# The pairs of experts of a mixture-of-experts stage written out, and the steps around a gated block put ahead of the weight splits

## The reference

```python
def moe_swiglu(x, router, w_gate, w_up, w_down):
    logits = (x @ router).astype(jnp.float32)
    top_vals, top_idx = lax.top_k(logits, TOP_K)            # 2 of 8 experts for each token
    gates = jax.nn.softmax(top_vals, axis=-1)
    combine = jnp.sum(jax.nn.one_hot(top_idx, N_EXPERTS) * gates[..., None], axis=-2)
    y = jnp.zeros_like(x)
    for e in range(N_EXPERTS):                              # w_gate[e], w_up[e]: 1024 x 3584
        y = y + combine[..., e:e + 1] * swiglu(x, w_gate[e], w_up[e], w_down[e])
    return y                                                # w_down[e]: 3584 x 1024
```

## Time and profile before

| | |
|---|---|
| median of 3 runs | 1626.28 us (1620.76, 1626.28, 1626.63) |
| the profiled execution | 1621.89 us, its span 1620.2 us |
| busy in the span | PE 94%, PEld 78%, DVE 78%, ACT 64%, POOL 8% |
| mean granted TensorE clock | 0.981 of full speed |
| traffic | 484 MB, of which HBM read 477 MB; 303 GB/s over the span |

### The profile page before, as it was taken

One profiled execution on the slowest core, in us unless ns is written; L12 is line 12 of the kernel. 1 busy time (PEld: TensorE's weight loads), 2 busy tenths in 40 slices (PEclk: granted clock), 3 DMA queues, 4 the chain that ended last, 5 costly groups with the idle time before them and its releaser, 6 DMA issues.

```text
span 1620.2 us, 21958 instructions
## 1 busy us (share of the span) xinstructions
PE 1517.1 (94%) x7866; PEld 1266.3 (78%) x7866; DVE 1257.4 (78%) x1228; ACT 1042.0 (64%) x984; POOL 126.8 (8%) x148
## 2 busy tenths in 40 slices
PE   9999999999999998899998999888999989999786
PEld 9888988888896797788776787776887766887664
DVE  5687475554647666789889989789988989988987
ACT  4574444443436453677888777888776978777664
POOL 3103010000104201000000000000000000000220
PEclk9999999999999999999999999999999999999888
DMA  9448856465565462799999999999999999999994
GB/s 355 167 131 247 299 185 218 130 221 195 169 198 184 140 208 75 268 374 340 412 403 409 409 376 383 350 403 391 410 365 382 355 403 386 405 358 385 346 368 152
DMA packets 164690, 484.28 MB, mean 299 GB/s; under 512 B 8352, under 2 KB 11456, under 8 KB 164576
## 3 DMA queue, kind: packets, MB, share of 16 engines
q1 hardware_dynamic: 155504, 454.06, 75.2%
q0 software_dynamic: 7440, 25.83, 4.9%
q10 hardware_dynamic: 1632, 2.88, 0.5%
HBM read 477.21 MB, written 13.92 MB: 303 GB/s over the span
## 4 chain that ended last, share of the span: by engine, by line
PE 61%; DVE 17%; issue 13%; ACT 5%; DMA 3%; POOL 1%; ACTq 0%; DVEq 0%; POOLq 0%
PE bank L428 8%; PE bank L430 8%; PE bank L429 8%; PE bank L461 7%; PE bank L463 6%; PE bank L462 6%; DVE w_lo L2200 6%; ACT w_hi L1232 3%; PE bank L451 2%; PE bank L454 2%; PE bank L453 2%; DMA c_add<-gate_rows 2%; DVE w_lo_more L2200 2%; DVE w_lo L1643 1%; PE bank L424 1%
## 5 line engine op out<-in xcount | busy, mean ns | idle before, releaser
L1232 ACT ACTIVATE w_hi<-raw 128x2048 fp32r<-128x2048 f32 (+1 forms) x322 | 606.7, 1894 | 224.9 <-PE bank L463 105.5
L2200 DVE TENSOR_TENSOR w_lo<-raw,w_hi 128x2048 fp32r<-128x2048 f32 x221 | 502.8, 2287 | 62.4 <-ACT w_hi L1232 55.7
L1643 DVE TENSOR_TENSOR w_lo<-raw,w_hi 128x2048 fp32r<-128x2048 f32 (+1 forms) x96 | 211.1, 2203 | 144.4 <-ACT w_hi L1232 144.0
L2200 DVE TENSOR_TENSOR w_lo_more<-raw,w_hi_more 128x2048 fp32r<-128x2048 f32 x63 | 144.0, 2285 | 17.6 <-ACT w_hi_more L1232 14.6
L461 PE MATMUL bank<-w_hi,xT_hi 128*128 128x512 f32 (+1 forms) x384 | 147.1, 383 | 0.1
L424 PE MATMUL bank<-w_hi,xe_two 128*128 128x512 f32 x304 | 128.3, 422 | 19.6 <-DVE w_lo L2200 19.1
L463 PE MATMUL bank<-w_hi,xT_lo 128*128 128x512 f32 (+1 forms) x384 | 144.6, 377 | 0.0
L462 PE MATMUL bank<-w_lo,xT_hi 128*128 128x512 f32 (+1 forms) x384 | 144.5, 376 | 0.0
L1232 ACT ACTIVATE w_hi_more<-raw 128x2048 fp32r<-128x2048 f32 x64 | 122.5, 1914 | 13.4 <-PE bank L430 8.4
L425 PE MATMUL bank<-w_lo,xe_two 128*128 128x512 f32 x304 | 124.5, 410 | 1.6 <-issue 1.5
L428 PE MATMUL bank<-w_hi,xe_hi 128*128 128x512 f32 x304 | 120.8, 397 | 1.9 <-DVE xe_lo L2033 1.7
(11 more groups left out here) (374 smaller groups left out, 3177.7 us busy)
## 6 DMA issues: line engine op xcount, KB each, us to landing
raw<-in_moe_w_gate_dram SPq DMA_DIRECT2D x112, 1024.0 KB, 8.0
raw<-in_moe_w_down_dram SPq DMA_DIRECT2D x96, 1024.0 KB, 7.9
raw<-in_moe_w_up_dram SPq DMA_DIRECT2D x80, 1024.0 KB, 8.5
raw_more<-in_moe_w_up_dram SPq DMA_DIRECT2D x32, 1024.0 KB, 8.3
raw<-in_mem_wkv_dram SPq DMA_DIRECT2D x16, 1024.0 KB, 5.2
raw_more<-in_moe_w_down_dram SPq DMA_DIRECT2D x16, 1024.0 KB, 7.6
raw<-in_c_w_in_dram SPq DMA_DIRECT2D x12, 1024.0 KB, 5.1
raw<-in_ffn_w_gate_dram SPq DMA_DIRECT2D x10, 1024.0 KB, 5.6
```

The source lines that it names most:

```text
L1232: return nc.scalar.activation(dst, src, ACT.Copy)
L1643: tt(w_lo[s][:, 0:n], raw[c % NRAW][:, 0:n], w_hi[s][:, 0:n].bitcast(F32), ALU.subtract).then_inc(lo_made, 1)
L2200: tt(w_lo[s][:, :], raw_exp[r][:, :], w_hi[s][:, :].bitcast(F32), ALU.subtract).then_inc(lo_made, 1)
```

## The change

It rewrites how the pairs are run; the arithmetic is the same.

- The loop over pairs is a Python loop: the six jobs stand one behind the other in the program of PE, ACT, DVE and POOL. `job` is `wide + 2 * i`, where `wide` is still read at run time. The loop around the first wide job stays.
- Within the pairs and z the slots go round by four without a break: 84 chunks of a pair are a multiple of four, and the w job starts two slots on (`slot_of`). Each step c splits exactly chunk c + 4 (`splits`).
- ACT and DVE do the steps of a gated block ahead of the step's splits. The multiplication itself returns the bank; the last subtraction counts up a semaphore `eT_two_made` of its own, for which PE's down projection waits.
- The table is loaded at the start of the first kind of job only.
- Turned tokens are written only in the form that the next job reads: `xe_hi`/`xe_lo` from an n job, `xe_two` from a w job.
- At the end of an n job ACT does the two copies; DVE adds one bank there and the other in step 1 of the w job. The write of these rows moves from step 2 to step 4, and the PE product that looks up the next tokens (line 857) from step 4 to step 6.

```diff
+        def slot_of(z, n):
+            return E_SLOT[n % EC if z == "" else (n + 2 * (z == "w")) % (NSPL + 1)]
+
+        def splits(z, c):
+            return E_SPLIT[c] if z == "" else [c + NSPL + 1]
-        C_WIDE_Y = 2
+        C_WIDE_Y = 4
-        C_INDEX, C_TURN, C_COMBINE = 4, 4 * EJ + 4, 4 * EJ + EK // CK + 2
+        C_INDEX, C_TURN, C_COMBINE = 6, 4 * EJ + 4, 4 * EJ + EK // CK + 2
...
-            with pe.Fori(0, PAIRS) as i:
-                job = pe.snap(wide + 2 * i)
-                expert(job, "n", True)
+            for i in range(PAIRS):
+                job = wide + 2 * i
+                expert(job, "n", True, i)
                 expert(job + 1, "w", False)
...
+                            if narrow:
+                                pe.wait_ge(sem("eT_two_made"), EJ * n_narrow + q // 2 + 1)
+                            else:
+                                wait_emptied(pe, f"{z}et{q // 2}", job)
...
-                nc.scalar.preload_act_table_set("silu_and_others")
+                if z == "":
+                    nc.scalar.preload_act_table_set("silu_and_others")
...
+                    if z == "n" and c == EC - 1:
+                        act.wait_ge(chunk_used, idx + 1)
+                        for i in (1, 0):
+                            act.wait_ge(sem(f"y_kept{i}"), 16 * job + 16)
+                            copy(y[0:HP, i * W:(i + 1) * W], bank_of(f"{z}ed{i}")[HP:P, :])\
+                                .then_inc(sem(f"y_low{i}"), 1)
...
-                    for n in E_SPLIT[c]:
-                        if n < EC or not last:
-                            w_split(n)
                     if c in C_HID:
...
                     if narrow and c in C_LOW:
-                        act.wait_ge(sem("e_mult"), EJ * n_narrow + j + 1)
+                        wait_emptied(act, f"{z}et{j}", job)
...
+                    for n in splits(z, c):
+                        if n < EC or not last:
+                            w_split(n)
...
-                        tt(e_mul[j % 2][:, :], bank_of(f"{z}et{j}")[:, W // 2:W], e_act[j % 2][:, :], ALU.mult)\
-                            .then_inc(sem("e_mult"), 1)
+                        empties(tt(e_mul[j % 2][:, :], bank_of(f"{z}et{j}")[:, W // 2:W], e_act[j % 2][:, :],
+                                   ALU.mult), f"{z}et{j}")
```

More of the change, by code:

```diff
@@ L885, in combine, with expert @@
                         .then_inc(filled[2 * half + t], 1)
-            def expert(job, z, narrow):
+            def expert(job, z, narrow, n_narrow=None):
                 claims[:], signals[:] = before[0], before[1]
@@ L1208, in _ @@
                 next_x(job)
-            with pool.Fori(0, PAIRS) as i:
-                job = pool.snap(wide + 2 * i)
+            for i in range(PAIRS):
+                job = wide + 2 * i
                 next_x(job)
@@ L1503, in _, with turned @@
             nc.scalar.activation(gap[:, :], gap[:, :], ACT.Exp).then_inc(sem("gap_exp"), 1)
[L1505 removed]
+            def turned(tag, job, z):
                 for half in range(2):
                     b = wait_filled(act, f"{tag}{half}", job)
[L1508 to L1514 removed]
+                    if z in ("", "w"):
+                        ins = copy(xe_two[:, 4 * half:4 * half + 4, 0:HP],
+                                   b[:, :].rearrange("p (k s) -> p k s", k=4)[:, :, 0:HP])
+                    if z != "w":
+                        ins = copy(xe_hi[:, 4 * half:4 * half + 4, :].rearrange("p k s -> p (k s)"), b[:, :])
+                    ins.then_inc(sem("xe_hi_made"), 1)
+            turned("xA", None, "first")
             split(N0 + NSPL)
@@ L1602, in _ @@
                 expert(job, "", False)
-            with act.Fori(0, PAIRS) as i:
-                job = act.snap(wide + 2 * i)
+            for i in range(PAIRS):
+                job = wide + 2 * i
                 expert(job, "n", True, i)
@@ L2021, in indexed, with turned @@
                 copy(got_i[:, :], b[:, 0:1]).then_inc(sem("index_made"), 1)
-            def turned(tag, job):
+            def turned(tag, job, z):
                 for half in range(2):
@@ L2062, in _ @@
             split(N0 + 1)
-            turned("xA", None)
+            turned("xA", None, "first")
             split(N0 + NSPL)
@@ L2184, in expert @@
                         nc.vector.nop().then_inc(emptied[fillings[f"{z}eu{j}"][0]], 1)
-                    for i in range(2):
-                        if c != EC - 1 or last or not narrow:
-                            continue
+                    if z == "n" and c == EC - 1:
                         dve.wait_ge(chunk_used, idx + 1)
-                        dve.wait_ge(sem(f"y_kept{i}"), 16 * job + 16)
-                        col, b = slice(i * W, (i + 1) * W), bank_of(f"{z}ed{i}")
-                        copy(y[0:HP, col], b[HP:P, :]).then_inc(sem(f"y_low{i}"), 1)
-                        dve.wait_ge(sem(f"y_low{i}"), n_narrow + 1)
-                        tt(y[0:HP, col], b[0:HP, :], y[0:HP, col], ALU.add).then_inc(sem(f"y_made{i}"), 1)
-                        dve.wait_ge(sem(f"y_made{i}"), job + 1)
-                        nc.vector.nop().then_inc(emptied[fillings[f"{z}ed{i}"][0]], 1)
+                        narrow_y(1, job, n_narrow)
+                    if z == "w" and c == 1:
+                        narrow_y(0, job - 1, n_narrow)
                     def w_split(n, job=job):
-                        r, s = n % NEXP, E_SLOT[n % EC]
+                        r, s = n % NEXP, slot_of(z, n)
                         dve.wait_ge(hi_made, N0 + n + 1 + EC * job)
@@ L2241, in expert @@
                     if c == C_TURN and not last:
-                        turned(f"{z}xB", job)
+                        turned(f"{z}xB", job, z)
                     if last and c == 2:
@@ L2253, in _ @@
                 expert(job, "", False)
-            with dve.Fori(0, PAIRS) as i:
-                job = dve.snap(wide + 2 * i)
+            for i in range(PAIRS):
+                job = wide + 2 * i
                 expert(job, "n", True, i)
-                expert(job + 1, "w", False)
+                expert(job + 1, "w", False, i)
             expert(wide + 2 * PAIRS, "z", True, PAIRS)
```

49 lines of the change are left out of this document (25 added, 24 removed).

## The result

| | before | changed |
|---|---|---|
| median of 4 runs | 1626.24 us (1620.76 to 1626.63) | 1582.11 us (1580.72 to 1583.29) |
| ratio | | 0.9736, 95% interval 0.9714 to 0.9758 |
| the profiled execution's span | 1620.2 us | 1579.0 us |

The change made the kernel 2.6% faster. Of the 41.2 us between the two profiled executions 41.1 lie between the first narrow job's first matmul and the end of the z job.

What follows compares the result with a forecast made beforehand. Narrow jobs bound by loads or DVE, wide by PE, z mostly by DVE. Stage 823.4 to 105 + 3 x 119.2 + 2 x 103.5 + 118.5 = 788.1, 35.3 less: 1586.6, plus half of 4.4, 1589 us; range 1576 to 1612.

Steps and rivals of the forecast that it cites:

- The w jobs: Three wide jobs: PE's stall at chunk 3 behind the y work goes; 119.2 us each, bounds 118.5 and 121.0.
- The second and third n job: Narrow jobs of 111.4 and 112.2 us: DVE and loads both limit near 100; 103.5 each, bounds 100.6 and 107.9.
- The first n job: First narrow job, 107.9 us, at the loads' pace: 105 forecast, bounds 103 and 107.9.
- only the joints: Rival: loads hold every n job at 107.9, so only the joints between jobs gain, 13.8 us; 1610 us, chance 0.18.
- The z job: Last job, 124.2 us with 15 us of DVE idle: 118.5 forecast, bounds 114 and 123.4.
- At nothing: Parts priced at zero: five table loads in ACT's slack, later token index and y rows, second y addition, splitting chunk c + 4.
- Straight code stalls: Rival: fetching the longer written-out program stalls engines at other places, joints give nothing; 1618 to 1626 us, chance 0.06.
- Gated steps hold the splits: Rival: ACT and DVE wait for PE's fold at gated blocks, queueing later splits; slower, 1642 at 1.2 us a block, chance 0.07.
- the signs that the prediction named: Expected: n 102 to 105, w 119 to 120, z below 120 us; ACT's `e_mul` wait below 10 us in all.
- the prediction's 18.6 us: ACT's gain from seven dropped table loads at the skill page's 2.66 us each; 9.0 by the profile, mostly covered.

Runs made afterwards that it cites:

- h1: The changed kernel with an n job's four y instructions all on DVE again, ahead of the subtraction of the w job's chunk 3: 1592.6 us, ratio 0.9813 to before.
- h2: The changed kernel with a table load at the start of each of the eight jobs again: 1587.6 us, ratio 0.9779 to before.
- g3: The changed kernel loading only half of each chunk in the three n jobs, which leaves out work the result needs: 1572.8 us.
- g4: The changed kernel with DVE subtracting only half of each chunk in the n jobs, which leaves out work the result needs: 1580.2 us.
- e2: The kernel before with only its loop over pairs written out: 1617.5 us, ratio 0.9954 to before.
- e3: The changed kernel with the splits again ahead of a gated block's steps on ACT and DVE: 1586.5 us, ratio 0.9772 to before.
- g1: The changed kernel with the old slot cycles of four and twice three put back: 1583.5 us, ratio 0.9756 to before.
- g2: The kernel before with its pairs written out and the new slots by four, nothing else: 1602.2 us, ratio 0.9859 to before.
- e1: The changed kernel with its pairs in a hardware loop again on PE, ACT, DVE and POOL: 1587.2 us, ratio 0.9777 to before.
- e4: The changed kernel with splits ahead of the gated steps and the bank returned by the last subtraction again: 1591.2 us, ratio 0.9811 to before.

## Why the prediction was right, and where not

Forecast 1589 us, range 1576 to 1612, 35.3 us off the stage; measured 1582.1 and 41.1. By its terms:

*The w jobs:* 119.2 forecast, 119.5 to 119.6 measured. The stall behind the four y instructions was the cause, as h1 shows by putting it back (PE idle at the same chunk). The table load, put back in h2, costs these jobs 0.7 to 0.8 us each, which the forecast had at nothing.

*The second and third n job:* 103.5 forecast, 102.7 and 102.6 measured. Loads and DVE both near 100 with the loads on top is what g3 and g4 found: 101.3 with DVE out of the way, 100.3 with the loads out of the way. But the way there was argued wrongly in two places. The ACT stall at the way back, 4.17 us and a load, was to be gained "behind" the joint; writing out alone (e2) left the n job at 111.0, so it had been covered. And the slots' cycles of three were "in the 103.5" without a price; alone they are the largest part, 16 us of the stage. I had looked at the gated blocks, where a wait with a name stands; e3 shows that in the n jobs the order gives nothing beyond the slots. In the changed kernel the gap of 2.56 us is removed twice, by the slots and, as g1's trace reads, by the order, and undoing one shows neither. So 103.5 was close by luck in part: the floor was judged rightly, the way there not. The token index was also "at nothing"; PE's gap there and the clock behind it are in the kernel before (3.2 us), in e2 and in g2, and gone in the changed kernel, without a price of their own.

*The first n job:* 105 forecast, 103.5 measured. I had said that it ran at the pace of its loads, since 407 GB/s for 107.9 us are 41.9 loads. The rate was full, but in that job of the kernel before no copy of ACT waited for a transfer, while in the changed kernel 14 do in the same job, at the same 407 GB/s (7.0 us in all). Some of the rate filled buffers for the w job, which then ran at 390 GB/s and threw the lead away. The same rate now carries the job in 103.5 us. A full rate in one stretch showed that the transfers did not stop there, and not that the job waited for them. The rival that was built on this step (only the joints, 1610) fell with it; e2, which takes away the joints alone, took 1617.5.

*The z job:* 118.5 forecast, 114.8 measured, the largest miss, 3.7 of the 5.8 us. I left DVE about half of its 15 us of idle time. It has 6.6 left. The order works there (5.0 us in z by e3), probably the slots too (2.7 by g1), and the table load with its gap of 1.1 us (h2).

*At nothing:* seven table loads. Two stood behind the unexplained wait, the others "where ACT had slack". h2 finds 5 to 6 us in the changed kernel; what they cost in the kernel before was not measured. The slack is an average over the job; at its start there is none.

*The rivals.* Straight code stalls: ACT's rows follow at once, no stretch grew. Gated steps hold the splits: ACT's wait for e_mul went from 31.6 to 15.9 us and no job is longer. Of the signs that the prediction named, this one failed all the same, since it wanted less than 10 us; the others (n, w and z, one table load, over 395 GB/s, no idle PE at the fold) came. What the Trainium skill says of taken branches ("Runtime: NRT & Kernel Launch", "Instruction fetch mechanics") fits PE, idle for 2.63 us at the way back in e1 and without a gap there in straight code; on ACT e1 has a branch and no such wait. Of the 2.66 us that the Trainium skill ("ScalarE: Activation LUTs", "What ACT_TABLE_LOAD costs") gives for a switch to a different set, the runs again show the 1.28 only; here the set that is loaded is the one in use, so that the prediction's 18.6 us took the figure beyond what it is stated for.

## What to carry to other kernels

When several fixes aim at one limit, undoing one of them in the finished kernel can measure almost nothing; add each to the kernel before as well. Only the pair of numbers (16 us alone, 2.5 us at the end, for the slots) tells what it did, and for the order, which has only the second number, it stays open. A stretch at full transfer rate is bound by it only if the copies wait for the landings; otherwise the rate is filling buffers for someone. And a ring of buffers that has to close on itself inside a loop body can cost more in its short cycles (16 us here) than the branch that one sees (4.9).

## What the runs showed of the hardware

- At a way back of a loop PE was idle for 2.1 to 2.6 us before the next matmul, in both kernels that have it, with a body of about 1005 matmuls. ACT's 4.17 us were seen in the kernel before and not in e1, which has the same loop without a table load behind the branch; open.
- Loads of 1 MB in a row kept 403 to 407 GB/s for 667 us, with a median time from issue to landing of 9.9 to 12.5 us, where it was 8 before: more in the queue, and a first n job at 407 GB/s both times.
- A load of the table that is already in use took ACT 1.28 us, and the next copy started 0.01 to 0.02 us behind it.
- PE's lower clock level was granted behind gaps of PE of 1.6 to 4.9 us, though not behind each of them (none behind the 2.56 us at 1074.17 in the kernel before, or the 1.95 us in e4). In the second n job the mean granted clock was 0.94 to 0.95 before and in e2 and g2, 0.98 in e1 with the one at its way back, and 1.00 in the other kernels.
